# A two-layer diffusion backbone on one core: rows of the 256-token stages begin 120 elements into their 512 instead of 112

## The chip, the core and the metric

The kernel runs on one core of a Trainium2 chip. The metric is the device time of one execution in microseconds, and the median of several runs counts. TensorE does the matrix products, ScalarE and VectorE the element-wise work, GpSimd a few sums, and DMA queues bring weights in from HBM.

## The reference

Two layers work on 256 latent tokens `x` and 256 context tokens `xc`, 1024 features each. In a layer a half-step SwiGLU is followed by two mixers side by side (grouped-query attention with sinks and a window, and a gated short convolution), whose outputs are merged with sigmoid gates, and then by a second half-step SwiGLU. Each part is preceded by an RMSNorm with shift and scale from a conditioning vector and followed by a gate.

```python
def swiglu(h, wi, wo):
    a, g = jnp.split(h @ wi, 2, axis=-1)
    return (jax.nn.silu(g) * a) @ wo

def gated_merge(o_attn, y_conv, ga, gb, w_oa, w_ob, w_out):
    m = jax.nn.sigmoid(ga) * (o_attn @ w_oa) + jax.nn.sigmoid(gb) * (y_conv @ w_ob)
    return m @ w_out
```

`wi` is 1024 x 5632, `wo` 2816 x 1024, `w_in` 1024 x 4352, `w_oa` and `w_ob` 512 x 1024, `w_out` 1024 x 1024, all float32. In the second (last) layer the context tokens are needed only for keys and values. After those nothing of the context is computed: attention output, merge and the second SwiGLU of that layer have 256 tokens where all before have 512.

## The kernel before, in words

Features lie on the 128 partitions, tokens along the free dimension. An activation tile such as `hH` is `[128, 8, 512]`: 8 blocks of 128 features, each a row of 512 tokens.

Every product of float32 matrices is made of three float32r products. ScalarE copies an operand to a float32r tile (the "high" part), VectorE subtracts it from the original (the "low" part), and TensorE adds up high x high, low x high and high x low in PSUM. `triple` (line 549) issues these three matmuls; they are lines 552, 553 and 554 of the profile. Each matmul holds a 128x128 block of the weights (`wH` or `wL`) in the array, loaded by an LDWEIGHTS of its own, and streams a row of an activation tile: `hH`, `hL` (normed activations, then the merged mixers), `QH`, `QL` (attention output), `YH`, `YL` (convolution output), `GH`, `GL` (SwiGLU product). The weights come in pieces of 128 x 1024 floats through a ring of four: SyncE issues the load, ScalarE makes `wH` (line 1005), VectorE `wL` (line 1266), and TensorE uses a piece in `columns_piece`, `rows_piece`, `last_rows` or `opening` (24 matmuls a piece at full width of 8 column blocks or 4 feature blocks by 2). Semaphores tie these steps: a piece waits for its low part, and the next load into a slot waits for the low part of the piece before it.

`span(t)` (line 81) gives the elements of a 512-element row that a stage of `t` tokens uses. For 512 tokens it is the whole row; for 256 it begins at `SHORT_AT`. `h_span` (line 321) does the same for the normed activations. The writers use the same slices as the matmuls: ScalarE at lines 1020, 1078, 1150, 1182 and 1219, VectorE at 1345, 1483, 1575, 1646 and 1699. Not all 256-column matmuls go by it: the products of the second layer's `w_in` other than keys and values stream elements 0 to 255 of rows that hold all 512 tokens (`columns_piece` without `cs`), and where a 512-token stage is done in two halves the halves begin at elements 0 and 256 (`side`). The stages that do begin at `SHORT_AT` are the second layer's `w_oa`, `w_ob`, `w_out` and its second SwiGLU.

The tiles that TensorE streams and the weight pieces are all placed a multiple of 128 elements apart in a partition; small padding tiles (`to_row`, `around_rows`) see to that.

The order of work on each engine is written out by hand; nothing is planned at run time. `keep_busy` (line 713) issues small matmuls whose results are not used, in the norms of 256 tokens.

Of the kernel before, what the change touches and what calls it, by code (L numbers as in the profile page):

```python
# [74 lines left out]
N_SOON = 2 * SEQ + P  # L75


SHORT_AT = 112


def span(t):

    at = SHORT_AT if t == SEQ else 0
    return slice(at, at + t)
# [58 lines left out]
def build(nc, x, c, ctx, c_ctx, w_ada, b_ada, norm_w, ffn1_wi, ffn1_wo, w_in, conv_w, sink, w_oa, w_ob, w_out,  # L143
          ffn2_wi, ffn2_wo, final_norm_w, consts, out):
    stack = ExitStack()
    with stack:
# [174 lines left out]
        def h_span(v, hf):  # L321

            at = hf * SEQ + (SHORT_AT if T_NORM[v] == SEQ else 0)
            return slice(at, at + SEQ)
# [1444 lines left out]
```

## Time and profile before

| | us |
|---|---|
| median of 3 runs | 1854.21 |
| lowest and highest | 1852.0, 1860.06 |
| the profiled execution, its own time | 1853.89 |
| its span, first to last instruction | 1852.0 |
| TensorE busy | 1827.1 (99%) |
| weight loads busy | 1550.1 (84%) |
| VectorE busy | 1124.0 (61%) |
| ScalarE busy | 692.3 (37%) |
| GpSimd busy | 101.0 (5%) |

The span is that of one profiled execution. A matmul's record lasts from its start to its last result, and consecutive matmuls overlap: a record of 0.28 us can be followed by the next after 0.12 us. The busy share is the union of these records. Ends of matmuls are modelled, starts are read.

### The profile page before, as it was taken

What the parts mean: (1) busy time and instruction counts of PE and PEld (TensorE: products, weight loads), DVE (VectorE), ACT (ScalarE), POOL (GpSimd) and SP (SyncE); (2) the same over time, 40 slices, a digit from 0 to 9 for tenths busy, and PEclk for the clock granted to TensorE, in tenths of its full rate; (3) what the DMA queues carried; (4) which work ended last, traced back from release to release, by engine and by line L of the source; (5) the groups of instructions that cost most, each with busy time, mean ns of one, the idle gap of its engine ahead of it and who ended that gap; (6) DMA issues with size and microseconds to landing.
All of it is one profiled execution on the core that took longest, in us unless ns stands there. A gap on an engine that the chain in (4) does not pass through costs nothing.

```text
span 1852.0 us, 26221 instructions
## 1 busy us (share of the span) xinstructions
PE 1827.1 (99%) x10099; PEld 1550.1 (84%) x10099; DVE 1124.0 (61%) x1503; ACT 692.3 (37%) x1086; POOL 101.0 (5%) x173
## 2 busy tenths in 40 slices
PE   7999999999999999999999999999999999999998
PEld 5788888888777789888888888888888899999998
DVE  4777736656654356877737557777322587576554
ACT  3433332234434324433332244333322465455542
POOL 1000001010000001000001010000000100000000
PEclk9999999999999999999999999999999999999999
DMA  8666536423222223566527435665223254546652
GB/s 313 214 190 185 163 99 218 156 70 102 80 78 71 81 91 126 182 189 188 157 91 236 139 114 181 184 192 159 91 93 100 69 154 140 154 134 205 192 193 91
DMA packets 183380, 271.48 MB, mean 147 GB/s; under 512 B 25228, under 2 KB 146556, under 8 KB 183292
## 3 DMA queue, kind: packets, MB, share of 16 engines
q1 hardware_dynamic: 164400, 202.99, 35.4%
q0 software_dynamic: 18432, 67.12, 11.8%
q8 instruction: 64, 1.05, 0.2%
q14 instruction: 24, 0.20, 0.0%
q10 hardware_dynamic: 460, 0.13, 0.0%
HBM read 269.16 MB, written 1.05 MB: 146 GB/s over the span
## 4 chain that ended last, share of the span: by engine, by line
PE 93%; DVE 3%; ACT 2%; issue 1%; DMA 0%; ACTq 0%; POOL 0%; DVEq 0%
PE ps L552 23%; PE ps L554 23%; PE ps L553 23%; PE turned L552 2%; PE turned L553 2%; PE turned L554 2%; PE scored L552 2%; PE scored L553 2%; PE scored L554 2%; PE ps L607 2%; PE ps L617 2%; PE ps L609 2%; PE turned L886 1%; PE scored L855 1%; PE turned L869 1%; PE scored L583 1%
## 5 line engine op out<-in xcount | busy, mean ns | idle before, releaser
L1266 DVE TENSOR_TENSOR wL<-raw,wH 128x1024 fp32r<-128x1024 f32 x364 | 443.6, 1223 | 450.8 <-ACT wH L1005 450.5
L552 PE MATMUL ps<-hH,wH 128*128 128x512 f32 (+1 forms) x1832 | 652.7, 356 | 0.6 <-ACT T L1071 0.6
L553 PE MATMUL ps<-hL,wH 128*128 128x512 f32 (+1 forms) x1832 | 646.2, 353 | 0.0
L554 PE MATMUL ps<-hH,wL 128*128 128x512 f32 (+1 forms) x1832 | 646.1, 353 | 0.0
L1005 ACT ACTIVATE wH<-raw 128x1024 fp32r<-128x1024 f32 x364 | 383.4, 1057 | 670.0 <-PE ps L554 664.1
L552 PEld LDWEIGHTS ps<-hH,wH 128*128 128x128 f32 x1832 | 344.8, 188 | 67.7 <-issue 19.6
L554 PEld LDWEIGHTS ps<-hH,wL 128*128 128x128 f32 x1832 | 344.8, 188 | 48.6
L553 PEld LDWEIGHTS ps<-hL,wH 128*128 128x128 f32 x1832 | 344.9, 188 | 46.7
L552 PE MATMUL ps<-GH,wH 128*128 (+2 forms) x376 | 131.5, 350 | 0.0
L553 PE MATMUL ps<-GL,wH 128*128 (+2 forms) x376 | 131.2, 349 | 0.0
L554 PE MATMUL ps<-GH,wL 128*128 (+2 forms) x376 | 131.2, 349 | 0.0
L1314 DVE SCALAR_TENSOR_TENSOR acc<-adaC,cact,acc 128x1024 f32<-128x1024 f32 x96 | 118.8, 1280 | 0.0
L1090 ACT ACTIVATE T<-ps 128x512 f32<-128x512 f32 (+1 forms) x88 | 43.1, 542 | 154.6 <-PE ps L554 148.9
L1078 ACT ACTIVATE GH<-T 128x512 f32 (+3 forms) x88 | 49.4, 579 | 113.5 <-DVE T L1475 113.5
L607 PE MATMUL ps<-hH,wH 128*128 128x256 f32 (+1 forms) x248 | 77.0, 331 | 7.8 <-ACT hH L1020 5.0
L554 PEld LDWEIGHTS ps<-GH,wL 128*128 128x128 f32 x376 | 70.8, 188 | 9.4
L553 PEld LDWEIGHTS ps<-GL,wH 128*128 128x128 f32 x376 | 70.8, 188 | 9.3
L552 PEld LDWEIGHTS ps<-GH,wH 128*128 128x128 f32 x376 | 70.7, 188 | 9.3
L524 POOL TENSOR_TENSOR T<-T 128x256 f32<-128x256 f32 x30 | 23.2, 773 | 973.4 <-ACT T L1010 972.4
L609 PE MATMUL ps<-hH,wL 128*128 128x256 f32 (+1 forms) x248 | 75.1, 322 | 0.0
L1475 DVE TENSOR_TENSOR T<-T 128x512 f32<-128x512 f32 (+1 forms) x88 | 50.8, 620 | 31.2 <-ACT T L1071 31.2
L1314 DVE SCALAR_TENSOR_TENSOR acc<-adaW,cact,acc 128x1024 f32<-128x1024 f32 x56 | 69.3, 1280 | 0.0
(222 smaller groups left out, 2172.3 us busy)
## 6 DMA issues: line engine op xcount, KB each, us to landing
raw<-in_ffn_wi SPq DMA_DIRECT2D x176, 512.0 KB, 3.7
raw<-in_ffn_wo SPq DMA_DIRECT2D x88, 512.0 KB, 3.3
raw<-in_w_in SPq DMA_DIRECT2D x60, 512.0 KB, 3.9
adaC<-in_w_ada POOLq DMA_DIRECT2D x48, 512.0 KB, 4.5
adaW<-in_w_ada POOLq DMA_DIRECT2D x32, 512.0 KB, 4.5
adaA<-in_w_ada POOLq DMA_DIRECT2D x24, 512.0 KB, 4.0
adaB<-in_w_ada POOLq DMA_DIRECT2D x24, 512.0 KB, 4.5
raw<-in_w_out SPq DMA_DIRECT2D x16, 512.0 KB, 3.4
```

The source lines that it names most:

```text
L552: mm(dst, wa, ra, start=start, stop=False, **kw)
L553: mm(dst, wa, rb, start=False, stop=False, **kw)
L554: return mm(dst, wb, ra, start=False, stop=stop, **kw)
L607: mm(ps[banks(j) + b][:, cols], wH[:, s, w], hH[:, kk, rows], start=(kk == 0 and cols.start == 0), stop=False, skip_group_check=True)
L609: mm(ps[banks(j) + b][:, cols], wL[:, s, w], hH[:, kk, rows], start=False, stop=False, skip_group_check=True)
L617: last = mm(ps[banks(j) + b][:, cols], wH[:, s, weights(j, kk % 4, b)], hL[:, kk, rows], start=False, stop=(kk == DC - 1), skip_group_chec ...
L1005: av(wH[:, s, :], raw[:, s, :], ACT.Copy).then_inc(hi_done, 1)
L1078: av(dst, T[:, 2 + b, 0:t], ACT.Copy).then_inc(g_hi, 1)
L1090: av(T[:, b, 0:t], ps[b][:, 0:t], ACT.Copy).then_inc(a_out, 1)
L1266: tt(wL[:, s, :], raw[:, s, :], wH[:, s, :].bitcast(F32), ALU.subtract).then_inc(lo_done, 1)
L1314: stt(dst[:, v, :], src, cact[:, v, k:k + 1], dst[:, v, :], ALU.mult, ALU.add).then_inc(acc_step, 1)
L1475: tt(T[:, 2 + b, 0:t], T[:, 2 + b, 0:t], T[:, b, 0:t], ALU.mult).then_inc(g_prod, 1)
```

## The change

The start of the 256-token rows within their 512 elements goes from 112 to 120, for those who write them and for the matmuls that stream them. Both lie within the row (120 + 256 = 376). The number and the order of instructions, their shapes and the DMAs stay as they are.

```diff
-SHORT_AT = 112
+SHORT_AT = 120
```

The two helpers that use it, unchanged:

```python
def span(t):
    at = SHORT_AT if t == SEQ else 0
    return slice(at, at + t)

def h_span(v, hf):
    at = hf * SEQ + (SHORT_AT if T_NORM[v] == SEQ else 0)
    return slice(at, at + SEQ)
```

## Rows read from the trace of the kernel before

**Rows 1.** Windows by stage: busy us (instructions) by engine, granted clock, DMA share, GB/s.
```profile
core 0: us, PE busy (x) PEld busy (x) DVE busy (x) ACT busy (x) POOL busy (x), PEclk, DMA share, GB/s
1602.00:1648.00 46.00, 44.32 (x388) 43.92 (x386) 32.62 (x58) 21.84 (x32) 1.81 (x3) 1.00 0.57 182
1648.00:1660.00 12.00, 11.26 (x82) 11.15 (x83) 6.10 (x16) 5.24 (x9) 0.60 (x1) 0.86 0.02 5
1700.00:1838.00 138.00, 137.96 (x1219) 137.79 (x1217) 74.24 (x90) 66.90 (x101) 2.23 (x3) 1.00 0.55 171
```
**Rows 2.** Waits of the weight loads, 1602 to 1852 us: total, times, longest.
```profile
PEld scored L552 <- DVE hL L1699: 1.2, 1, 1.2
PEld ps L552 <- DVE wL L1266: 0.8, 1, 0.8
PEld ps L607 <- DVE wL L1266: 0.3, 1, 0.3
```
**Rows 3.** Timeline, rows that begin at element 112: start us, us, engine, line.
```profile
1720.02 0.28 PE L553 MATMUL ps<-hL,wH 128*128 128x256 f32 x1
...
1723.42 0.28 PE L553 MATMUL ps<-hL,wH 128*128 128x256 f32 x1
```
**Rows 4.** Timeline, 256 columns from element 0, 24 rows.
```profile
1580.12 0.28 PE L552 MATMUL ps<-hH,wH 128*128 128x256 f32 x1
...
1582.88 0.28 PE L554 MATMUL ps<-hH,wL 128*128 128x256 f32 x1
```
**Rows 5.** Timeline, 256 columns from element 256, 8 rows.
```profile
1465.35 0.28 PE L553 MATMUL ps<-GL,wH 128*128 128x256 f32 x1
...
1466.19 0.28 PE L554 MATMUL scored<-GH,wL 128*128 128x256 f32 x1
```
**Rows 6.** Timeline, 512 columns from element 0, 16 rows.
```profile
1292.75 0.39 PE L553 MATMUL ps<-hL,wH 128*128 128x512 f32 x1
...
1296.15 0.39 PE L553 MATMUL ps<-hL,wH 128*128 128x512 f32 x1
```
**Rows 7.** Timeline of weight loads under matmuls of 2 and 128 columns.
```profile
1648.71 0.52 PEld L732 LDWEIGHTS scored<-cst,T 128*128 128x128 f32 x4 [1.56 <-DVE X L1353]
1649.15 0.53 PEld L732 LDWEIGHTS scored<-cst,sqT 128*128 128x128 f32 x4
1649.60 1.20 PEld L717 LDWEIGHTS ps<-cst 128*128 128x128 f32 x10
1650.72 0.53 PEld L732 LDWEIGHTS scored<-cst,sqT 128*128 128x128 f32 x4
```
**Rows 8.** Timeline of weight loads, eight transposes and the load behind them.
```profile
1593.48 0.90 PEld L869 LDWEIGHTS turned<-cst,T 128*128 128x128 f32 x8
1594.35 0.19 PEld L552 LDWEIGHTS ps<-hH,wH 128*128 128x128 f32 x1
```
**Rows 9.** Groups by line and shape, 1602 to 1852 us: busy us, mean ns, idle before.
```profile
L1005 ACT ACTIVATE wH<-raw 128x1024 fp32r<-128x1024 f32 x79 | 83.0, 1058 | 60.7 <-PE ps L554 60.7
L1078 ACT ACTIVATE GH<-T 128x256 f32 x16 | 6.2, 418 | 9.5 <-DVE T L1475 9.5
L1266 DVE TENSOR_TENSOR wL<-raw,wH 128x1024 fp32r<-128x1024 f32 x79 | 96.2, 1225 | 77.2 <-ACT wH L1005 77.1
L1483 DVE TENSOR_TENSOR GL<-T,GH 128x256 f32 x18 | 7.0, 426 | 3.4 <-ACT GH L1078 3.4
```
**Rows 10.** Timeline, start 0, just behind transposes, 9 rows.
```profile
1594.58 0.28 PE L553 MATMUL ps<-hL,wH 128*128 128x256 f32 x1
...
1595.29 0.28 PE L553 MATMUL ps<-hL,wH 128*128 128x256 f32 x1
1595.40 0.28 PE L554 MATMUL ps<-hH,wL 128*128 128x256 f32 x1
1595.53 0.28 PE L552 MATMUL ps<-hH,wH 128*128 128x256 f32 x1
```

## The prediction

> **What bounds the kernel now.** I read the table of stages first, since the change touches one part of the program only: the 256-token stages of the second layer, which begin with w_oa at 1602 us. In them TensorE is busy nearly all the time at a granted clock of 1.00, the upper of its two levels, 2.4 GHz [rows 1]; the one hole is the norm at 1648 to 1660 us. ScalarE and VectorE work 67 and 74 us of the 138 us from 1700 to 1838, and the DMA engines are 0.55 busy. The waits say the same: from 1602 us the weight loads of the plain matmuls waited 2.3 us in all for VectorE (1.2 + 0.8 + 0.3, [rows 2]). So the end is set by how closely one matmul follows the last, and the change is worth what it does to that distance.
>
> The busy column can't show the distance, because matmuls overlap. I take it from the timeline, start to start. From 1720.02 to 1723.42 us, in a stage that begins its rows at element 112, stand 30 intervals [rows 3]: 3.40 / 30 = 113.3 ns, or 272 periods of the 2.4 GHz clock. From 1580.12 to 1582.88 us, matmuls of the same 256 columns that begin at element 0 stand 23 intervals apart in all [rows 4]: 2.76 / 23 = 120.0 ns, 288 periods. Rows that begin at element 256 have the same 120.0 ns (0.84 us in 7 intervals, [rows 5]), and 512 columns from element 0 take 3.40 / 15 = 226.7 ns, 544 periods [rows 6]. One column a period explains 256 and 512 of these. The surplus is 32 periods at start 0 and 256, whatever the length, and 16 at start 112. The start is thus a real lever, and it works on a fixed cost per matmul.
>
> **How many matmuls.** From the loops: w_oa and w_ob 4 pieces each of 8 column blocks of 3 matmuls, 96 + 96; w_out 8 such pieces, 192; the opening of the second feed-forward 96; its other 40 pieces of wi 24 each, 960; 22 pieces of wo 24 each, 528. The sum is 1968. The trace agrees: 1219 in the 138 us of the long stage [rows 1] is 113.2 ns for one. One nanosecond per matmul is worth 1.97 us of the run, one clock period 0.82 us.
>
> **The parts.** (a) The streamed operand. The new start moves every one of these 1968 streams by 8 elements, 32 bytes. Starts on record are 0, 112 and 256 only, so the price of 120 must be bounded. From below, the next thing that ends late is the weight load, one of 128x128 per matmul. Where almost nothing streams (2 columns) or 128 columns do, 18 loads take 1650.72 - 1648.71 = 2.01 us, 111.7 ns each, 268 periods [rows 7]. Those weights are plain f32 and the pieces here f32r; the size is the same, and no row shows the f32r load as the one that ends last. The lower bound is then 1968 x (111.7 - 113.3 ns) = -3.3 us. A farther floor is the eight 128x128 loads of the transposes, 1594.35 - 1593.48 = 0.87 us, 109 ns each [rows 8], which would be -8.5 us. From above, the nearest row is the 120.0 ns of start 0: 1968 x 6.67 ns = +13.1 us. Nothing forbids a start that no row shows from being worse than both; as many periods above start 0 as start 112 lies below it would be 126.7 ns, +26.2 us.
>
> Which value? The three surpluses fit a stream handled in runs of 32 elements in which the first run costs its own length again: start 112 is 3 x 32 + 16 and its first run has 16 elements, surplus 16; start 0 and 256 have 32, surplus 32. Start 120 leaves a first run of 8, 256 + 8 = 264 periods, which is under the 268 of the weight load, so the load ends last and the gain is cut to -3.3 us. I take this value as the likeliest single one; it ends on a measured row (the load's 268 periods) 4 periods from where the kernel is, and the trace doesn't prove it.
>
> (b) What writes those rows. ScalarE's copies into hH, GH, QH, YH and VectorE's differences into hL, GL, QL, YL go to the same new start. They are 128x256 operations of 418 and 426 ns [rows 9] and lie beside TensorE's work, except where a stage opens: TensorE waits 1.2 us for the last differences before w_out [rows 2], and the opening of the second feed-forward follows the eight blocks of the norm. If a write to the new start cost 10% more, some 42 ns, on these eight blocks, that would be 0.3 us. I cost it at 0, with 0.3 us either way. (c) Weights, DMAs, semaphores, the order of instructions and the bytes moved stay. A TensorE faster by 1.7 ns a matmul wants a piece every 24 x 111.7 = 2.68 us instead of 2.72 us; a piece costs ScalarE 1.06 us and VectorE 1.22 us [rows 9], so nothing else becomes late. Sum: -3.3 + 0 = -3.3 us on the profiled execution's 1853.89 us, 1850.6; that execution lies 0.3 us under the median of the three runs, so the forecast is 1850.9 us.
>
> The Trainium skill weighs against any such lever. TensorE: Matmul & The Clock Gate, section "Wait — 56ns, not 53.3ns?", gives start to start as N / 2.4 GHz plus about 2.5 ns, with no term for the address. By that rule 256 columns would be an estimated 109.2 ns at every start; the trace's 120.0 and 113.3 ns differ, so the measurement decides. If the surplus did fall to what the page states, the change would give about 8 us, an estimate.
>
> **The rivals.** *No change.* If the lever has steps of 16 elements or more, 112 and 120 lie in one step and the median stays, 1854.2 us. For it: all surpluses seen are multiples of 16, and a first distance after a pause is not a clean one either: just behind transposes, between 1594.58 and 1595.53 us, the distances at start 0 average 0.95 / 8 = 119 ns with single ones of 110 to 130 before 120 returns [rows 10], so loads and streams settle into a common beat. Against: no row tests a smaller step. The Trainium skill's SBUF — State Buffer, Door 1, has 16-byte lines with full speed from two hits a line; 448 and 480 bytes are both whole lines, so by that rule too nothing would change.
>
> *The last run counts, not the first.* At start 112 first and last run have 16 elements, at start 0 both 32, so the rows cannot tell which one costs. At start 120 the last run has 24: 280 periods, 116.7 ns, 1968 x 3.33 ns = +6.6 us, 1860.8 us.
>
> *The gain of 112 is lost.* The stream at 112 begins on a multiple of 16 elements (64 bytes), at 120 it doesn't. If that is the unit in which rows are fetched, 256 elements touch 17 units instead of 16, and one unit more is 272 + 16 = 288 periods: 120.0 ns, +13.1 us, 1867.3 us. This is the rival on the other side; it decides as soon as the distance reaches 116 ns. For it: 32 and 16 are whole units, which fits as well as runs of 32. Against: nothing in the rows shows a start off such a multiple. *Worse than start 0*, by the bound above, 126.7 ns: 1880.4 us.
>
> *A lower floor than the load's.* If the f32r load is quicker than the plain one, 109 ns: 1845.7 us.
>
> **How the numbers follow.** Less surplus, stopped by the weight load, 1850.9 us: 0.33. No change, 1854.2: 0.22. Gain of 112 lost, 1867.3: 0.20. Last run counts, 1860.8: 0.16. Worse than start 0, 1880.4: 0.06. Lower floor, 1845.7: 0.03. The likeliest alone would be 1849 to 1853. Cases of both signs hold much of the chance, so the range takes in the 120 ns case with its spread and the load's floor: 1848.5 to 1868.5 us; the last two cases, 0.09, stay outside. What a measurement here can tell from no change is about 0.5%, 9.3 us or 4.7 ns a matmul. Faster by more than that needs a distance under 108.6 ns: 0.02. Slower by more: the 120 ns case, the one worse and a little of the 116.7 ns case, 0.27. Within it: 0.71.
>
> **What would show it.** In the profile after, 30 intervals of the long feed-forward stage: 3.35 us means the load's floor, 3.40 no change, 3.50 the last run, 3.60 the fetch unit. Distances in the stages of start 0 must stay at 120.0 and 226.7 ns, the first 1602 us must not move, and the difference of the spans must be 1968 times the difference of the distances. If the distances stay at 113.3 ns and the span moves, or the writers' durations change by more than 20 ns, my account of the change is wrong.

## The result: 0.38% slower, by a longer distance between matmuls

| | us |
|---|---|
| before, median of 20 runs | 1853.88 (1851.85 to 1861.56) |
| changed, median of 20 runs | 1861.78 (1860.39 to 1864.20) |
| ratio, 95% interval | 1.0038 (1.0030 to 1.0047) |
| profiled execution after, its own time and its span | 1862.13, 1860.2 |

The forecast was 1850.9 us. The measured time lies inside the range of 1848.5 to 1868.5, on the other side of the kernel before.

The windows by stage of the changed kernel answer to [rows 1]; columns as there.
```profile
core 0: us, PE busy (x) PEld busy (x) DVE busy (x) ACT busy (x) POOL busy (x), PEclk, DMA share, GB/s
1602.00:1648.00 46.00, 45.13 (x381) 44.84 (x379) 32.30 (x56) 20.93 (x30) 1.37 (x2) 1.00 0.57 181
1700.00:1838.00 138.00, 138.00 (x1168) 138.00 (x1168) 70.71 (x82) 64.84 (x96) 0.00 (x0) 1.00 0.55 174
```
TensorE is as busy as before at the same granted clock, and in the same 138 us it starts 1168 matmuls where it started 1219. The timeline shows each of them further from the last; its first and last row of 31 answer to [rows 3].
```profile
1719.93 0.28 PE L553 MATMUL ps<-hL,wH 128*128 128x256 f32 x1
...
1723.48 0.28 PE L553 MATMUL ps<-hL,wH 128*128 128x256 f32 x1
```
3.55 us in 30 intervals are 118.3 ns, 284 periods of 2.4 GHz, where it was 113.3. And the distance is no longer even:
```profile
1730.11 0.28 PE L552 MATMUL ps<-hH,wH 128*128 128x256 f32 x1
1730.23 0.28 PE L553 MATMUL ps<-hL,wH 128*128 128x256 f32 x1
1730.35 0.28 PE L554 MATMUL ps<-hH,wL 128*128 128x256 f32 x1
1730.46 0.28 PE L552 MATMUL ps<-hH,wH 128*128 128x256 f32 x1
1730.58 0.28 PE L553 MATMUL ps<-hL,wH 128*128 128x256 f32 x1
1730.70 0.28 PE L554 MATMUL ps<-hH,wL 128*128 128x256 f32 x1
```
It goes 0.12, 0.12, 0.11, 0.12, 0.12 us, single distances between 115 and 123 ns. The groups by line and shape say that the writers of the rows did not change (durations 418 and 426 ns in [rows 9]):
```profile
L1078 ACT ACTIVATE GH<-T 128x256 f32 x16 | 6.1, 418 | 9.5 <-DVE T L1475 9.5
L1483 DVE TENSOR_TENSOR GL<-T,GH 128x256 f32 x18 | 7.0, 425 | 3.4 <-ACT GH L1078 3.4
```
From the first matmuls of each stage in both traces the difference comes together: w_oa and w_ob 21.8 to 22.7 us, w_out 24.7 to 25.2, the norm 7.65 both times, opening and wi 121.3 to 126.1, wo 60.05 to 62.56, the last norm 8.6 to 8.9. That is 9.0 us; the 1602 us ahead of them were 0.9 us shorter in this execution, and the span grew by 8.2. 1968 x 5.0 ns would be 9.8 us. Half of w_out's share vanished in two waits of TensorE that became shorter, for VectorE inside the stage (1.0 to 0.9 us) and for GpSimd behind it (1.4 to 1.2 us). And the first 60 or so matmuls of the opening were not at 113.3 ns in the kernel before. Its timeline there, ahead of a short pause at 1663.7 us and behind it:
```profile
1662.13 0.28 PE L607 MATMUL ps<-hH,wH 128*128 128x256 f32 x1
...
1663.19 0.28 PE L609 MATMUL ps<-hH,wL 128*128 128x256 f32 x1
...
1665.30 0.28 PE L607 MATMUL ps<-hH,wH 128*128 128x256 f32 x1
...
1667.34 0.28 PE L607 MATMUL ps<-hH,wH 128*128 128x256 f32 x1
```
9 intervals of 117.8 ns (1.06 us), then 18 of 113.3 ns (2.04 us), with the same instructions on rows that begin at 112. The experiments show what that is.

### The profile page after: what moved, and what is told of

Same layout as the page of the kernel before. It is cut to its first block, busy times and chain, and to the rows that moved or that the text cites. A ratio compares the mean times of both kernels' runs of the same rounds, so it can differ in the third digit from the quotient of the medians.

```text
span 1860.2 us, 26221 instructions
## 1 busy us (share of the span) xinstructions
PE 1836.7 (99%) x10099; PEld 1559.0 (84%) x10099; DVE 1124.4 (60%) x1503; ACT 692.1 (37%) x1086; POOL 101.1 (5%) x173
## 4 chain that ended last, share of the span: by engine, by line
PE 93%; DVE 3%; ACT 2%; issue 1%; DMA 0%; ACTq 0%; POOL 0%; DVEq 0%
PE ps L552 23%; PE ps L554 23%; PE ps L553 23%; PE turned L552 2%; PE turned L554 2%; PE turned L553 2%; PE scored L552 2%; PE scored L553 2%; PE scored L554 2%; PE ps L607 2%; PE ps L617 2%; PE ps L609 2%; PE turned L886 1%; PE scored L855 1%; PE turned L869 1%; PE scored L583 1%
## 5 line engine op out<-in xcount | busy, mean ns | idle before, releaser
L552 PE MATMUL ps<-hH,wH 128*128 128x512 f32 (+1 forms) x1832 | 654.5, 357 | 0.4 <-ACT T L1071 0.4
L552 PEld LDWEIGHTS ps<-hH,wH 128*128 128x128 f32 x1832 | 345.0, 188 | 67.7 <-issue 19.6
L552 PE MATMUL ps<-GH,wH 128*128 (+2 forms) x376 | 131.8, 351 | 0.0
L552 PEld LDWEIGHTS ps<-GH,wH 128*128 128x128 f32 x376 | 70.9, 189 | 9.3
```

What stands on the lines that cost most here:

```text
L552: mm(dst, wa, ra, start=start, stop=False, **kw)
```

## The experiments

Four theories stood against each other. A: a stream's surplus over one column a period is a function of its own start (my forecast's view). B: TensorE's two readers, of the streamed rows and of the weights, disturb each other, and the distance between their addresses counts. C: a fetch unit of 16 elements. D, formed after the first runs: B, with the readers settling into one of a few beats. A beat is here a sequence of distances that repeats for as long as TensorE streams on.

**Map of starts.** Behind the last matmul of the kernel before (here and in the next two runs):

```diff
+            pe.wait_ge(fin_out, 4)
+            for start, n, shift in PROBE:
+                for j in range(16):
+                    w = slice(shift + j % 7 * P, shift + (j % 7 + 1) * P)
+                    triple(ps[j % 8][:, 0:n], wH[:, 0, w], wL[:, 0, w], rowsH[:, start:start + n],
+                           rowsL[:, start:start + n], True, True, False)
```

> The kernel before with 4608 more matmuls behind its last one: the same high/low triples of 256 columns, 48 at each start, starts 0, 4, ..., 252 of a row and then 248, 240, ..., 0; the weight slices as in the kernel. Theory A (each stream's surplus over 256 clock periods is a fixed function of its own start, by runs of 32 elements): starts 0, 32, 64, ... all 120.0 ns, 16, 48, 80, 112 all 113.3 ns, 120 and 24, 56, 88 all 118.3 ns, the same pattern eight times. Theory B (TensorE's two readers, of the streamed rows and of the weights, get in each other's way, and what counts is the distance of their starts in a longer period, 128 elements or more): 112 differs from 16, 48 and 80; the pattern repeats every 128 elements or not at all. Theory C (a fetch unit of 16 elements): every start that is a multiple of 16 other than multiples of 32 at 113.3 ns, all others the same among themselves. Where the second pass gives another value at a start than the first, the distance depends on what ran before and is a beat that locks in, not a property of the start.

Distances in ns, each worked out over the last 36 intervals of its streak from the starts in the trace:

```
start       64    68    72    76    80    84    88    92    96   100   104   108   112   116   120   124
upward   120.0 118.6 116.7 118.3 117.8 120.0 120.0 113.3 118.6 118.7 117.4 119.3 113.3 119.3 118.4 117.1
downward 120.0       116.7       113.3       120.0       118.7       118.7       117.8       118.3
```

The upward pass had the same values at 128 to 188 and at 192 to 252, to 0.1 ns: the pattern repeats every 64 elements, 256 bytes. Theory A's run of 32 elements falls (120.0 at 64, 118.6 at 96), C falls (the multiples of 16 differ). Theory B had its period wrong: it was put at 128 elements or more, with 112 unlike 48, and these two are alike. And starts 80, 104 and 112 have two values. The timeline at start 16, which answers to 80, first upward, then downward, 33 rows each:
```profile
1880.59 0.28 PE L553 MATMUL ps<-hH,wH 128*128 128x256 f32 x1
...
1884.36 0.28 PE L555 MATMUL scored<-hH,wL 128*128 128x256 f32 x1
...
2384.20 0.28 PE L553 MATMUL ps<-hH,wH 128*128 128x256 f32 x1
...
2387.83 0.28 PE L555 MATMUL scored<-hH,wL 128*128 128x256 f32 x1
```
3.77 / 32 = 117.8 ns and 3.63 / 32 = 113.4 ns for the same instructions on the same addresses. So the price is not a property of the start alone.

**Map of weights.**

> The kernel before with 4608 more matmuls behind its last one: triples of 256 columns at row starts 0, 112 and 120, 48 at each of 32 places of the weight slice, 0, 4, ..., 124 elements into the piece (128 columns each). Theory A and theory C (the stream's own start alone decides): 120.0, 113.3 and 118.3 ns at every place of the weights, 32 equal values three times. Theory B (the distance of the two readers decides): shifting the weights moves the distance; start 0 with weights at 16 (or at 112) elements has 113.3 ns, start 112 with weights at 112 has 120.0 ns, and the three curves are one curve displaced by 112 and 120 elements.

Rows from the timeline, 33 rows for each pair: row start 0 with the weight slice 16 elements on; start 112 with weights at 0; start 112 with weights at 112; start 120 with weights at 0; start 120 with weights at 8.
```profile
1879.23 0.28 PE L553 MATMUL ps<-hH,wH 128*128 128x256 f32 x1
...
1882.86 0.28 PE L555 MATMUL scored<-hH,wL 128*128 128x256 f32 x1
...
2037.78 0.28 PE L553 MATMUL ps<-hH,wH 128*128 128x256 f32 x1
...
2041.41 0.28 PE L555 MATMUL scored<-hH,wL 128*128 128x256 f32 x1
...
2196.36 0.28 PE L553 MATMUL ps<-hH,wH 128*128 128x256 f32 x1
...
2200.20 0.28 PE L555 MATMUL scored<-hH,wL 128*128 128x256 f32 x1
...
2219.11 0.28 PE L553 MATMUL ps<-hH,wH 128*128 128x256 f32 x1
...
2222.90 0.28 PE L555 MATMUL scored<-hH,wL 128*128 128x256 f32 x1
...
2230.40 0.28 PE L553 MATMUL ps<-hH,wH 128*128 128x256 f32 x1
...
2234.03 0.28 PE L555 MATMUL scored<-hH,wL 128*128 128x256 f32 x1
```
Over 32 intervals: 113.4, 113.4, 120.0, 118.4 and 113.4 ns. Shifting the weights by 8 elements gives start 120 the distance of 112 back; shifting them by 112 takes it from start 112. Of the 96 combinations all twelve whose distance (row start less weight start) is 16 or 48 beyond a multiple of 64 had 113.3 ns. This much of theory B stands: the distance of the two readers decides, and no row start is good by itself. For weights moved by multiples of 8 elements the curves of the three row starts are one curve displaced. With weights on odd multiples of 4 the three curves still agree with one another at equal distances, but no longer with the map of starts: row start 0 with weights at 36 is at distance 28 and had 120.0 ns, where rows at 92 with weights at 0, at the same distance, had 113.3. So the distance alone is the whole rule only for weights moved in steps of 8 elements.

**Map of widths.**

> The kernel before with 4608 more matmuls behind its last one: 512 columns at starts 0, 4, ..., 128; 256 columns at every start from 100 to 132; and starts 0, 112, 120 with 128, 192, 224, 240, 248, 264, 272, 288, 320, 384 columns, 48 each. Theory A with the surplus by the first run: at 512 columns the same surplus as at 256, so 226.7 ns at start 0 and 220.0 at 112, and at start 112 a surplus of 16 periods at all widths over 272. With the surplus by the last run: it changes with the width at one start. Theory B (the readers meet only while weights are read, some 256 periods): surplus at 512 columns not more than at 256. A floor by the weight load shows as one distance, about 111.7 ns, at 128, 192 and 224 columns.

At 128, 192 and 224 columns all three starts have 111.7 ns. The first and last of 33 rows at 128 columns:
```profile
2412.59 0.28 PE L553 MATMUL ps<-hH,wH 128*128 128x128 f32 x1
...
2416.16 0.28 PE L555 MATMUL scored<-hH,wL 128*128 128x128 f32 x1
```
3.57 / 32 = 111.6 ns, the distance of the plain f32 loads in [rows 7]. Three widths with one distance say that the stream doesn't end last there; that it is the f32r weight load is the likely reading, and no run has it apart. But at 256 columns nothing in the three maps came under 113.3 ns, 33 single starts from 100 to 132 among them. With 512 columns the surplus is 32 periods (226.7 ns) at starts 60, 64, 124 and 128 and up to 51 elsewhere (234.6 ns at 52; 233.3 at 112 and at 120): the kernel's 512-column stages, at distance 0 with 226.7 ns, are at a place as good as any tried for their width, while at 256 columns the same distance costs 120.0 ns.

Both expectations on the surplus failed here. Theory A wanted 220.0 ns for 512 columns at start 112 and got 233.3. Theory B let the readers meet only while weights are read, so the surplus was not to grow with the width; at start 112 it grew from 16 periods at 256 columns to 48 at 512. What of B is left is that the distance counts, not how the surplus comes about.

**Streams alone at 120.** The matmuls that stream hH and hL read 8 elements beside where the rows are written (they compute with rows 8 tokens aside).

```diff
+READ_AT, WRITE_AT = 120, 112
-                        last = chunk(both, kk, side(hf), h_span(v, hf), ...)
+                        last = chunk(both, kk, side(hf), h_span_r(v, hf), ...)
...
```

> In the second layer the matmuls that stream hH and hL in 256-token stages (w_out, the opening and wi of the second SwiGLU, 1248 of the 1968) begin at 120 while ScalarE and VectorE write these rows at 112 as before, so they multiply rows 8 tokens aside; everything else begins at 112. Theory: the streams alone lose, 118.3 instead of 113.3 ns in these stages, and the whole gets 1248 x 5.0 ns = 6.2 us longer, less what waits absorb, near 1859.5 us. Rival: the writers at 120 disturb the streams (or are slower themselves); then the distances stay at 113.3 ns and the time at 1854 us.

Median 1860.0 us against 1860.1 for the kernel before, ratio 1.0005 (0.9992 to 1.0018): no difference, where 6 us were expected. The trace shows why. The first pair is from wi (start 120, 32 rows), the second from wo (start 112, 31 rows):
```profile
1739.72 0.28 PE L575 MATMUL ps<-hL,wH 128*128 128x256 f32 x1
...
1743.39 0.28 PE L576 MATMUL ps<-hH,wL 128*128 128x256 f32 x1
...
1799.75 0.28 PE L576 MATMUL scored<-GH,wL 128*128 x1
...
1803.28 0.28 PE L576 MATMUL turned<-GH,wL 128*128 x1
```
3.67 / 31 = 118.4 ns as expected, and 3.53 / 30 = 117.7 ns where 113.3 was expected. Start 112 runs at 117.8 ns here, and the kernel before did so too on this occasion: 9 of its 13 runs took 1859.7 us or more, where in the first comparison 15 of 20 took under 1855. The kernel before has two times, and the beat after the pause in wi, shown next, makes nearly all of the difference.

**When a beat is chosen.** The timeline of the map of widths, in its part that is the kernel before, has the switch in it: rows before and after the one wait of TensorE in wi.
```profile
1667.83 0.28 PE L553 MATMUL ps<-hH,wH 128*128 128x256 f32 x1
...
1670.09 0.28 PE L555 MATMUL ps<-hH,wL 128*128 128x256 f32 x1
1670.98 0.38 PE L553 MATMUL ps<-hH,wH 128*128 128x256 f32 x1 [0.61 <-ACT T L1080]
1671.20 0.28 PE L554 MATMUL ps<-hL,wH 128*128 128x256 f32 x1
...
1674.50 0.28 PE L555 MATMUL ps<-hH,wL 128*128 128x256 f32 x1
```
20 intervals of 113 ns (2.26 us) before it, 28 of 117.9 ns (3.30 us) after it, and 117.8 ns from there to the end of wo 170 us later. The beat changes at a pause of 0.61 us, and nearly 1500 matmuls behind it are 4.4 ns longer each, 6.5 us. In the profile of the kernel before, the same wait was followed by 113.3 ns, and the switch stood at another place: its opening began at 117.8 ns, where the opening of this run had 113.3.

**Map with pauses.**

```diff
+            for n, (start, width) in enumerate(PROBE):
+                pe.wait_ge(probe_b, n) if n > 0 else None
+                stream(start, 12)
+                mm(ps[0][:, 0:P], ident, cst[:, 0:P], ...).then_inc(probe_a, 1)
...
+                av(T[:, 3, 0:width], T[:, 2, 0:width], ACT.Copy).then_inc(probe_b, 1)
```

> The kernel before with, behind its last matmul, 112 streaks of 36 matmuls of 256 columns, 14 streaks for each of the row starts 112, 16, 92, 28, 120, 123, 124, 0; before each streak TensorE waits for a ScalarE copy of a width that changes from streak to streak, so that every streak sets out anew. Theory D (the two readers settle into one of a few beats that repeat for as long as TensorE isn't interrupted, and the distance of the starts says which are to be had): at 112 and 16 some streaks at 113.3 and others at 117.8 ns, at 0 all at 120.0, at 120 all at 118.3 ns; 92 and 28 either always 113.3 or again two values. Theory A with noise: one value per start, 113.3 at 112 in all 14.

Measured over the last 18 intervals of each streak: start 92, 14 of 14 at 113.3; start 28, 14 of 14 at 113.3; 112, 13 of 14 at 113.3 (the first began with distances of 213 ns, the lower level of the granted clock, and was still settling); 16, 14 of 14 at 117.8; 120 at 118.1 to 118.3; 123 at 115.6; 124 at 116.9 to 117.4; 0 at 120.0. A miss in part: I expected a mixture at 112 and 16 and each kept one value, so these pauses did not throw the dice. They differed by up to 0.35 us in length, but what ran ahead of each was the same, and the distances behind them were the same within about 1 ns from one streak to the next. In the map of starts, where another start ran ahead, 16 had 113.3 ns in one of its two streaks. What sets the beat at a pause stays open. For use it is enough that 28 and 92, with weights at 0, gave one value under all pauses.

**Weights moved aside in the real kernel.**

```diff
-SHORT_AT = 112
+SHORT_AT = 120
+        sb("aside", [P, 8])
         raw = sb("raw", [P, RING, PIECE])
-        sb("to_row", [P, 95])
+        sb("to_row", [P, 87])
```

> SHORT_AT = 120 as in the changed kernel, and a pad of 8 elements ahead of the tiles raw, wH and wL (taken from the pad to_row), so that the weights lie 8 elements further on and the rows don't. Theory B and D (the distance between stream and weights counts): the 256-token stages are at distance 112 again and run at 113.3 or 117.8 ns instead of 118.3, while all 512-column matmuls come to distance -8, for which the map of widths has 233.3 instead of 226.7 ns: some 6500 of these lose 6.7 ns, the whole some 40 us longer, near 1900 us. Theory A or C (the start alone): 118.3 ns in the 256-token stages as in the changed kernel, 226.7 ns at 512 columns, the whole 1862 us.

1893.5 us in its one run, where 1900 was expected, and 1862 if the start alone counted. First and last of 27 rows of a 512-token stage (wo of the first layer):
```profile
1099.83 0.40 PE L553 MATMUL turned<-GH,wH 128*128 x1
...
1105.90 0.40 PE L555 MATMUL turned<-GH,wL 128*128 x1
```
6.07 / 26 = 233.5 ns where [rows 6] have 226.7: 512-column matmuls whose own start was not touched lose 6.7 ns, because the weights moved. In the 256-token stages w_oa and w_ob ran at 113.3 ns and wi and wo at 117.8, the two beats of distance 112, with rows at 120.

**Start 0.**

```diff
-SHORT_AT = 112
+SHORT_AT = 0
```

> SHORT_AT = 0, the plain start. One beat of 120.0 ns at distance 0 in every map, so 1968 x 6.67 = 13.1 us over the best runs of the kernel before: near 1865 us with little scatter, and 3 us over the changed kernel's 1861.8.

1864.1 us (1863.4 to 1865.5, 6 runs), ratio to the kernel before 1.0051 (1.0032 to 1.0070), distance 120.0 ns throughout. About 1865 was expected.

**Start 92, twice.**

```diff
-SHORT_AT = 112
+SHORT_AT = 92
```

> SHORT_AT = 92. By the map, the beat at distance 28, 92, 156 and 220 was 113.3 ns each time it was tried. If that is the only beat there, the kernel is at 1852 to 1854 us in every run, where the kernel before falls to 1860 in part of its runs: 0.2 to 0.3% faster on the mean. If 92 has a second beat too (theory D in its full form), the runs scatter as before. Theory A (odd starts cost): 118.4 ns as at 120, 1861 us.

> SHORT_AT = 92 once more, on the same chip as the three others of this call. One beat, 113.3 ns: 1851.5 to 1855.5 us in every run, no run near 1860, however many of the kernel before fall there on this chip.

First: 1853.4 us (1851.5 to 1855.6, 12 runs) against 1853.9 (1851.7 to 1861.0, 19 runs), ratio 0.9995 (0.9984 to 1.0005). The 0.2 to 0.3% expected on the mean did not come, it was 0.06%: only 3 of those 19 runs of the kernel before were over 1857.4 us. Again, on another chip: 1853.6 us (1851.6 to 1854.9, 5 runs) against 1860.7 (1857.5 to 1861.6, 21 runs), ratio 0.9966 (0.9952 to 0.9979). None of 17 runs came near 1860. Rows of wi in the second:
```profile
1739.91 0.28 PE L552 MATMUL ps<-hH,wH 128*128 128x256 f32 x1
...
1743.31 0.28 PE L552 MATMUL ps<-hH,wH 128*128 128x256 f32 x1
```
3.40 us in 30 intervals from one L552 to the other, 113.3 ns: the good beat, also on the chip where each of the kernel before's 21 runs was over 1857.4 us.

The runs of start 92 still lie 4 us apart, and a second cause, which is not the beat, makes most of that: the two profiled ones differ by 3.6 us. In the norm at 1648 us, which opens with a wait of TensorE of 1.4 us, the granted clock was 1.00 (2.4 GHz) throughout in the second trace and fell to its lower level (1.2 GHz) for a part of it in the others: its mean was 0.78 in the kernel before and in the changed one, and 0.64 in the first trace of start 92. From its first matmul to the opening's first the norm lasted 6.0, 7.65 and 9.3 us. The comparison of the two profiled kernels is free of it (7.65 us in both).

**The changed kernel on that chip.** No edit.

> The changed kernel once more, on the same chip as its rivals: 118.3 ns, 1860.4 to 1864.2 us as before, 0.4% over start_92_again; against the kernel before anything from 0.1 to 0.5% slower, by how many of its runs fall into the slow beat of start 112.

1861.7 us (1860.2 to 1864.1), as the first time. Against the kernel before, now at 1860.7, it is 1.0011 (1.0002 to 1.0021). It is 0.44% over start 92. The change's price is what the kernel before had to lose: 118.3 ns against 113.3 in one beat, against 117.8 in the other.

**Writers alone at 120.** The edit of the streams with the two numbers exchanged (`READ_AT, WRITE_AT = 112, 120`; rows again 8 tokens aside).

> ScalarE and VectorE write the 256-token rows of hH and hL at 120, the matmuls stream them from 112 as before (so they multiply rows 8 tokens aside). If the writers have no part in it: distances of 113.3 or 117.8 ns at those matmuls, durations of 418 and 420 ns for the writers as before, and the time of the kernel before within 0.1%, both kernels scattering alike. If writing at 120 cost anything: slower than the kernel before by more than that.

Ratio 0.9997 (0.9987 to 1.0006), distances 113.3 ns in w_out, 117.8 in wi, and the writers, from the groups by line:
```profile
L1241 ACT ACTIVATE hH<-GB 128x256 fp32r<-128x256 f32 x8 | 3.2, 415 | 8.1 <-DVE GB L1717 8.1
L1721 DVE TENSOR_TENSOR hL<-GB,hH 128x256 fp32r<-128x256 f32 x8 | 3.4, 421 | 0.4 <-ACT hH L1241 0.2
```
415 and 422 ns in the kernel before. Where the rows are written has no part in it.

**A version that beats both.** Start 92, and the rows of the second layer's w_in stage, which [rows 4] show at distance 0, laid 28 elements aside.

```diff
+            return h_rows[:, at:at + DC * TOK].rearrange("p (m t) -> p m t", m=DC)
+        hH, hL = h_tile(0, 0), h_tile(1, 0)
+        hH4, hL4 = h_tile(0, ASIDE), h_tile(1, ASIDE)
...
-                        last = triple(..., hH[:, kk, cs], hL[:, kk, cs],
+                        last = triple(..., (hH4 if aside else hH)[:, kk, cs], (hL4 if aside else hL)[:, kk, cs],
```

> SHORT_AT = 92, and the normed rows of the second layer's w_in stage lie 28 elements further on (hH and hL as one tile with room at its end), so that its 768 matmuls of 256 columns, at 120.0 ns in the kernel before, come to distance 28 as well. Theory D: 113.3 ns there, 768 x 6.67 = 5.1 us less; its 96 matmuls of 512 columns (keys and values) go from 226.7 to the 231.1 ns of the map, 0.4 us more. The whole 4.7 us under start_92, near 1848.7 us, and faster than the kernel before. If the distance didn't matter there: 1853.4 us as start_92.

1850.3 us (1848.7 to 1851.1, 5 runs), ratio to the kernel before 0.9948 (0.9934 to 0.9962), and 3.3 us under start 92 on the same chip. From the timeline of the w_in stage, 29 rows:
```profile
1576.82 0.28 PE L559 MATMUL ps<-h_rows,wH 128*128 128x256 f32 x1
...
1579.99 0.28 PE L560 MATMUL ps<-h_rows,wL 128*128 128x256 f32 x1
```
3.17 / 28 = 113.2 ns where it was 120.0. The stage became 2.8 us shorter, not 4.7: attention's matmuls break into it every 24 or 48 matmuls, and after each, five to ten distances average 118 to 119 ns before the beat sets in, some 180 in the stage.

## Why the prediction was wrong

The bound was right: TensorE's distance from start to start, 1968 matmuls, one nanosecond 2 us. So were the count, the floor of 111.7 ns, that the writers cost nothing, that nothing else becomes late, and that distances at start 0 and at 512 columns would not move.

The step that failed is "the three surpluses fit a stream handled in runs of 32 elements in which the first run costs its own length again". It gave 264 periods for start 120, hidden under the load's 268; measured are 284. The forecast's -3.3 us became +8.2 us between the two profiled executions. Three points, surpluses 32, 32 and 16, had been made a law of the start, when they were points of a pattern of 64 elements in the distance between two readers; the map of weights shows it. The rival by the last run named a number near the truth (116.7 ns, 1860.8 us) by luck, since the map of starts refutes its mechanism; and the range held because it had been drawn around cases of both signs. The rival of the fetch unit said 120.0 ns and is refuted too.

Two things in the rows, and one that I passed over in the trace, spoke against a law of the start alone. [Rows 10] showed distances at start 0 that took eight matmuls to settle; a cost fixed by the start would have been there at once. I used them as an argument for "no change" and not against the law. And the kernel before had runs at 1852.0, 1854.2 and 1860.1 us: three runs with a gap of 6 us, which is 4.4 ns on the matmuls after the pause. I took the median and did not ask what made the third. And the profile had both distances at start 112 in it, 117.8 and 113.3 ns in one opening, as shown in the section on the result; my working went by one place of the long stage.

The Trainium skill would not have pointed to two readers either. SBUF — State Buffer, "Who interferes with whom", gives TensorE two SBUF read ports, one for the streamed operand and one for the weight load, independent, and lets it wait on nobody. The runs differ: moving only the weights by 8 elements changed the distance of the matmuls from 118.4 to 113.4 ns, so here the two reads are not independent, and the measurement decides. Where and how they disturb each other, the runs don't say.

## What to carry to other kernels

Where every matmul has a weight load of its own, read the distance from start to start in the timeline and divide by the columns; a surplus that is not the same in all stages is worth a map of addresses, behind the kernel's last instruction, with the weights' address varied as well as the rows'. Two or three points of such a map are not a law. If a kernel's runs fall into two groups, find which distance differs between them before judging any small change against its median.

## What the runs showed of the hardware that was not expected

- The distance of float32r matmuls, each with its own 128x128 weights, depends on the distance in a partition between streamed rows and weights (exactly so for weights moved by multiples of 8 elements), with a period of 64 elements (256 bytes): 113.3 to 120.0 ns at 256 columns for multiples of 4 elements, up to 123.3 ns among single ones (start 129), and 226.7 to 234.6 ns at 512.
- The same instructions on the same addresses have more than one stable beat: 113.3 or 117.8 ns at distances 16 and 48 beyond a multiple of 64, 117.4 or 118.7 at 40. In the traces a beat lasted until TensorE paused or another start or another kind of matmul came. Row starts 28, 92, 156 and 220 with weights at multiples of 64 showed one beat alone, in 32 streaks and in the 17 runs of start 92.
- Which beat the kernel before gets differs between occasions: 5 of 20, 10 of 13, 3 of 19 and 21 of 21 runs over 1857.4 us in the four comparisons, which ran on different chips at least in the last three. Whether the chip decides it was not tried.
